# Halves of the probabilities in one matmul in all heads, and a new order of the stick-breaking work on VectorE

## What is computed

```
def stick_breaking_attention(q, k, v):
        z = jnp.einsum('bqhd,bshd->bhqs', qb, kf) * dh ** -0.5
        causal = (spos[None, :] < tpos[:, None])[None, None]
        log_beta = jax.nn.log_sigmoid(z)
        log_keep = jnp.where(causal, log_beta - z, 0.0)
        between = lax.cumsum(log_keep, axis=3, reverse=True) - log_keep
        a = jnp.where(causal, jnp.exp(log_beta + between), 0.0)
        return jnp.einsum('bhqs,bshd->bqhd', a, vf).astype(q.dtype)
```

## Time and profile before

| | |
|---|---|
| median of three runs | 738.01 us (737.94 to 738.75) |
| the profiled execution | 738.18 us, its span 736.4 us |
| TensorE clock granted, mean | 0.999 of full |
| TensorE matmul busy | 729.9 us, 99% of the span |
| VectorE busy | 595.8 us, 81% |
| ScalarE busy | 466.1 us, 63% |
| GpSimd busy | 257.9 us, 35% |

### The profile page before, as it was taken

How to read it: one execution, slowest core, us unless ns; L and a number is a source line. 1 busy time by engine, 2 the same in 40 slices (tenths; PEclk the granted TensorE clock), 3 DMA queues, 4 the chain that set the end, 5 groups by cost and what they waited for, 6 DMA issues and landing times.

```text
span 736.4 us, 11132 instructions
## 1 busy us (share of the span) xinstructions
PE 729.9 (99%) x3881; PEld 628.3 (85%) x3881; DVE 595.8 (81%) x838; ACT 466.1 (63%) x733; POOL 257.9 (35%) x204
## 2 busy tenths in 40 slices
PE   9999999999999999999999999999999999999997
PEld 7788888888888888888888999999999999888885
DVE  4979989978766777359998888888888888985787
ACT  5764177777858667654484756666666666764664
POOL 6837265976777878421003400000000000043201
PEclk9999999999999999999999999999999999999999
DMA  9662444222304223269971023333333354999914
GB/s 332 191 180 63 143 124 115 57 58 58 107 16 130 65 72 101 71 175 288 260 197 38 1 71 100 115 114 114 114 103 91 93 169 157 343 174 207 212 35 115
DMA packets 111520, 95.21 MB, mean 129 GB/s; under 512 B 3696, under 2 KB 91768, under 8 KB 111480
## 3 DMA queue, kind: packets, MB, share of 16 engines
q1 hardware_dynamic: 104920, 78.96, 34.5%
q0 software_dynamic: 6368, 15.73, 11.6%
q10 hardware_dynamic: 192, 0.01, 0.0%
HBM read 84.97 MB, written 4.73 MB: 122 GB/s over the span
## 4 chain that ended last, share of the span: by engine, by line
PE 97%; DVE 2%; issue 1%; ACT 0%; POOL 0%; POOLq 0%; DVEq 0%
PE ps L1060 13%; PE ps L1147 12%; PE ps L712 11%; PE ps L713 11%; PE ps L714 11%; PE ps L1066 6%; PE ps L734 6%; PE ps L983 4%; PE ps L775 3%; PE ps L1050 3%; PE ps L1048 3%; PE ps L1049 3%; PE ps L922 2%; PE ps L934 2%; PE ps L1003 1%; PE ps L907 1%
## 5 line engine op out<-in xcount | busy, mean ns | idle before, releaser
L712 PE MATMUL ps<-h_both,w_hi 128*128 128x512 f32 (+1 forms) x288 | 110.6, 384 | 0.0
L713 PE MATMUL ps<-h_both,w_hi 128*128 128x512 f32 (+1 forms) x288 | 109.1, 379 | 0.0
L714 PE MATMUL ps<-h_both,w_lo 128*128 128x512 f32 (+1 forms) x288 | 109.1, 379 | 0.0
L1950 POOL DMA_DIRECT2D w_a<-in_w_down x12 | 15.3, 1533 | 249.7 <-DMA w_a<-in_w_down 227.4
L1864 POOL TENSOR_TENSOR w_lo<-raw,w_hi 128x1024 fp32r<-128x1024 f32 x30 | 78.3, 2612 | 29.9 <-ACT w_hi L1343 29.5
L714 PEld LDWEIGHTS ps<-h_both,w_lo 128*128 128x128 f32 x288 | 54.2, 188 | 10.2
L713 PEld LDWEIGHTS ps<-h_both,w_hi 128*128 128x128 f32 x288 | 54.3, 189 | 8.9
L712 PEld LDWEIGHTS ps<-h_both,w_hi 128*128 128x128 f32 x288 | 54.3, 188 | 9.0
L1147 PE MATMUL ps<-wr_hi,xd_hi 128*128 128x512 f32 x154 | 60.0, 389 | 0.0
L1147 PE MATMUL ps<-wr_lo,xd_hi 128*128 128x512 f32 x154 | 59.9, 389 | 0.0
L1147 PE MATMUL ps<-wr_hi,xd_lo 128*128 128x512 f32 x154 | 59.9, 389 | 0.0
(11 more groups left out here) (337 smaller groups left out, 2074.6 us busy)
## 6 DMA issues: line engine op xcount, KB each, us to landing
raw<-in_w_in SPq DMA_DIRECT2D x40, 512.0 KB, 4.5
raw<-in_w_gate_up SPq DMA_DIRECT2D x24, 512.0 KB, 3.9
raw<-in_w_gate_up SPq DMA_DIRECT2D x40, 256.0 KB, 4.3
w_a<-in_w_down SPq DMA_DIRECT2D x9, 768.0 KB, 6.1
w_a<-in_w_down POOLq DMA_DIRECT2D x9, 768.0 KB, 10.7
s<-in_w_out SPq DMA_DIRECT2D x3, 768.0 KB, 8.2
w_a<-w_a POOLq DMA_DIRECT2D x3, 768.0 KB, 13.4
x_t<-in_first SPq DMA_DIRECT2D x8, 256.0 KB, 6.7
```

What stands on the lines that cost most here:

```text
L712: mm(acc, whi_c, a_hi_, start=first, stop=False, skip_group_check=further)
L713: mm(acc, whi_c, a_lo_, start=False, stop=False, skip_group_check=further)
L714: return mm(acc, wlo_c, a_hi_, start=False, stop=last, skip_group_check=further)
```

## The change

Three things. `MERGED` goes, and with it the form of `attend` and of `sum_out` that heads 0 to 3 had: all heads take six matmuls and two additions. On VectorE `kept_after(i + 1)` goes behind `turned_lo(i)`, for the stick-breaking heads. And the last two rounds of the top-k stand behind heads 1 and 3 instead of 0 and 1 (`LAST_ROUNDS`), the mask behind head 5 (`MASK_AFTER`) instead of head 2.

```diff
--- before.py
+++ after.py
@@ -88,10 +88,12 @@
 
 
 FIRST_FILL = 16
-MERGED = 4
 STEPS = (5, 8, 1)
 ROUNDS = TOPK // 8
 FIRST_ROUNDS = 13
+
+LAST_ROUNDS = (1, 3)
+MASK_AFTER = 5
 SHARE = 256
 
 
@@ -99,11 +101,6 @@
 
     first = FIRST_FILL + i * sum(STEPS) + sum(STEPS[:part])
     return first, first + STEPS[part]
-
-
-def outs_added(heads):
-
-    return heads + max(0, heads - MERGED)
 
 
 def tiles_ended(first, end):
@@ -912,7 +909,7 @@
 
             pe.wait_ge(probs_done, i + 1)
             if i:
-                pe.wait_ge(att_out_done, outs_added(i))
+                pe.wait_ge(att_out_done, 2 * i)
             else:
                 pe.wait_ge(va_kept, TB)
                 pe.wait_ge(vb_kept, TB)
@@ -927,18 +924,11 @@
             pe.wait_ge(v_hi_done, i // 2 + 1)
             pe.wait_ge(v_lo_done, i // 2 + 1)
             pe.wait_ge(a_lo_done, i + 1)
-            if i >= MERGED:
-
-                for k, half, first in ((0, 0, 0), (0, 1, HALF), (3, 1, 3 * P), (1, 0, P), (1, 1, HALF), (2, 1, HALF)):
-                    a, n = PACK[TB - k] + first - k * P, (half + 1) * HALF - first
-                    ins = mm(out_bank(half)[:, :, HALF - n:HALF], v_both[:, i % 2, k, :], a_both[:, :, a:a + n],
-                             start=k == 0, stop=k == half + 1, skip_group_check=True)
-            else:
-                for k in range(TB):
-                    n, a = (TB - k) * P, PACK[TB - k]
-                    for p, pr in enumerate((a_hi, a_lo)):
-                        ins = mm(z(1, k * P, S), v_both[:, i % 2, k, :], pr[:, a:a + n],
-                                 start=k == 0 and p == 0, stop=k == TB - 1 and p == 1, skip_group_check=True)
+
+            for k, half, first in ((0, 0, 0), (0, 1, HALF), (3, 1, 3 * P), (1, 0, P), (1, 1, HALF), (2, 1, HALF)):
+                a, n = PACK[TB - k] + first - k * P, (half + 1) * HALF - first
+                ins = mm(out_bank(half)[:, :, HALF - n:HALF], v_both[:, i % 2, k, :], a_both[:, :, a:a + n],
+                         start=k == 0, stop=k == half + 1, skip_group_check=True)
             ins.then_inc(out_done, 1)
 
         fill(0, 6)
@@ -1393,16 +1383,13 @@
 
             sc.wait_ge(out_done, i + 1)
             if i:
-                sc.wait_ge(att_out_done, outs_added(i))
-            if i >= MERGED:
-                run(att_rest.rearrange("p (x n) -> p x n", x=2), out_banks(slice(HD, P), 0), ACT.Copy).then_inc(att_rest_done, 1)
-            else:
-                run(att_rest[:, :], ps[HD:P, 5, :], ACT.Copy).then_inc(att_rest_done, 1)
+                sc.wait_ge(att_out_done, 2 * i)
+            run(att_rest.rearrange("p (x n) -> p x n", x=2), out_banks(slice(HD, P), 0), ACT.Copy).then_inc(att_rest_done, 1)
 
         def out_hi(i):
 
             r, chunk = slice(HD * (i % 2), HD * (i % 2) + HD), (i // 2 + PAIRS) % KC
-            sc.wait_ge(att_out_done, outs_added(i + 1))
+            sc.wait_ge(att_out_done, 2 * (i + 1))
             run(o_hi[r, chunk, :], att_out[r, :], ACT.Copy).then_inc(o_hi_done, 1)
 
         def gate(slot):
@@ -2179,14 +2166,11 @@
             ve.wait_ge(att_rest_done, i + 1)
             if 2 <= i:
                 ve.wait_ge(o_lo_done, i - 1)
-            if i >= MERGED:
-                rest = att_rest.rearrange("p (x n) -> p x n", x=2)
-                tt(rest, out_banks(slice(0, HD), HALF), rest, ALU.add).then_inc(att_out_done, 1)
-                ve.wait_ge(att_out_done, outs_added(i) + 1)
-                tt(att_out[r, :].rearrange("p (x n) -> p x n", x=2), out_banks(slice(0, HD), 0), rest,
-                   ALU.add).then_inc(att_out_done, 1)
-            else:
-                tt(att_out[r, :], ps[0:HD, 5, :], att_rest[:, :], ALU.add).then_inc(att_out_done, 1)
+            rest = att_rest.rearrange("p (x n) -> p x n", x=2)
+            tt(rest, out_banks(slice(0, HD), HALF), rest, ALU.add).then_inc(att_out_done, 1)
+            ve.wait_ge(att_out_done, 2 * i + 1)
+            tt(att_out[r, :].rearrange("p (x n) -> p x n", x=2), out_banks(slice(0, HD), 0), rest,
+               ALU.add).then_inc(att_out_done, 1)
 
         def rest_out(i):
 
@@ -2207,12 +2191,11 @@
         best_eight(FIRST_ROUNDS)
         k_rest(2)
         for i in range(ALL):
-            if i + 1 < HEADS:
-                kept_after(i + 1)
-            elif i + 1 < ALL:
+            if HEADS <= i + 1 < ALL:
                 logits_and_max(i + 1)
             turned_lo(i)
             if i + 1 < HEADS:
+                kept_after(i + 1)
                 break_probs(i + 1)
             elif i + 1 < ALL:
                 normalise(i + 1)
@@ -2220,10 +2203,9 @@
                 k_rest(i + 3)
             if i < ALL - 1:
                 sum_out(i)
-            r = FIRST_ROUNDS + 1 + i
-            if r < ROUNDS:
-                best_eight(r)
-            elif r == ROUNDS:
+            if i in LAST_ROUNDS:
+                best_eight(FIRST_ROUNDS + 1 + LAST_ROUNDS.index(i))
+            elif i == MASK_AFTER:
                 mask_the_rest()
         rest_out(ALL - 2)
         sum_out(ALL - 1)
```

## The result

The changed kernel takes 743.88 us, the median of six runs (742.48 to 747.24), beside 738.43 for the kernel before (six runs, 737.94 to 740.26). The ratio is 1.0075 [1.0063, 1.0087]: slower by 5.5 us, well outside the 0.2%. The forecast was 744.4, with a range of 741 to 748.

A forecast was written before the change was run, and what follows sets the result against it. TensorE was taken to bound the kernel, until VectorE's new loop with GpSimd outlasts a head. Waits of 2.0 + 5.0 less 0.56 for the merge gave +6.4 us on 738.01: 744.4, range 741 to 748.

The forecast's parts named there:

- The loop: Transposes, `a_hi`, `turned_lo`, scan, `break_probs`, `k_rest`, `sum_out`, next transposes: 10.37 us undisturbed, 14.34 with GpSimd, against TensorE's 13.10.
- three insertions: GpSimd's `q_lo`, `o_lo`, `w_lo` hold up scan, `break_probs`, `k_rest` by 0.91, 0.98, 2.08 us: together 3.97, with 2.73 spare.
- 1.24 each in loops 2 to 5: TensorE's wait at the transposes in each of these loops, 4.96 us together.
- 2.0 in loop 1: Transposes of head 2 come at 142.56 instead of 140.55 us: TensorE waits 2.0 us.
- the scan waits for `q_lo`: VectorE's scan behind `turned_lo` is held by GpSimd's `q_lo`, 2.39 - 1.48 = 0.91 us per loop.
- only some loops wait: Rival: two of five loops escape waiting, about 742 us; 8 in 100.
- third rival: More goes wrong: loop 6 waits 1.2 to 1.7 us, six TensorE restarts cost 0.2 each; 747.3 us, 12 in 100.
- VectorE pays for it: For the merged matmul in heads 0 to 3, `sum_out` becomes two instructions instead of one, 1.40 us in all.
- The rounds and the mask: Moved on VectorE, they cost nothing; if cover were gone, 0.7 us in two heads, and at most 1.2 for the mask.
- Loop 0: `k_rest` and `sum_out` end at 127.2, TensorE wants it at 127.45: no wait, by 0.2 us.
- Loop 6: Only one short piece of GpSimd's bias-and-mask sum comes between, costed at nothing; 1.2 us more if all held `k_rest`.
- The clock: Rival: clock falls during TensorE's pauses, one head at half clock adds 13 us, 757 us; 2 in 100.

The follow-up runs named there:

- the scan ahead: Changed kernel with `kept_after(i + 1)` ahead of `turned_lo(i)` again, six matmuls and late rounds kept: 738.78 us.
- `k_rest` last: Changed kernel with `sum_out(i)` ahead of `k_rest(i + 3)`, run twice: 738.25 and 738.66 us.
- `q_lo` late: Changed kernel where GpSimd's `q_lo` also waits for `a_lo_done` of head i, i from 1 to 6, so the scan comes first: 739.18 us.
- nudged kernel: Changed kernel with an 8x32 memset and a wait for it ahead of the scan in the loops of heads 1 and 2: 747.84 us.
- the order alone: Kernel before with only the scan moved behind `turned_lo`, eight matmuls and one addition in heads 0 to 3, rounds as before: 742.51 us.
- the changed kernel's second: The changed kernel run again, nothing altered, for another profile of its waits: 743.58 us.
- the merge alone: Kernel before with `MERGED = 0`, so six matmuls and two additions in all heads, order and rounds as before: 740.7 us.
- both: Changed kernel with the scan ahead of `turned_lo` again and `sum_out` ahead of `k_rest` as well: 738.22 us.

## Why the prediction was right, point by point

**The mechanism was right.** The loop, its three insertions, and the place of the wait came as worked out. In the loops of heads 3 to 5 the records are 3.50 to 3.73, 2.33 and 2.78 against 3.74, 2.46 and 2.77 in the sum, and the waits behind them 1.27, 1.43 and 1.26 against 1.24. It is shown from three sides: with the scan ahead or `k_rest` behind nothing waits, and with `q_lo` behind 0.2 us of 4.0 is left.

**Two terms of the sum were mis-sized.** The sum gave 6.4 us, all of it in the heads' stage, and that stage grew by 4.2. First, "1.24 each in loops 2 to 5" and "2.0 in loop 1": loops 1 and 2 did not wait, which takes 3.2 us off. The step that failed is "the scan waits for `q_lo`", taken from head 5 for all loops. The kernel before already showed the difference, on GpSimd in heads 1 and 5:

```profile
128.41 4.38 POOL L1864 TENSOR_TENSOR w_lo<-raw,w_hi 128x1024 fp32r<-128x1024 f32 x1 [4.92 <-ACT w_hi L1343]
132.92 2.37 POOL L1757 TENSOR_TENSOR q_lo<-proj,q_twice 64x512 fp32r<-64x512 f32 x1
...
181.23 2.40 POOL L1864 TENSOR_TENSOR w_lo<-raw,w_hi 128x1024 fp32r<-128x1024 f32 x1 [3.63 <-ACT w_hi L1343]
```

In head 5 that `w_lo` is over at 183.63, and GpSimd is idle for 0.32 us before `q_lo` (183.95 in the earlier trace rows); in head 1 `q_lo` follows a `w_lo` without a pause. In the changed kernel's heads 1 and 2 that `w_lo` ends just too late. Head 6 has such a pair too, and there `q_lo` is ahead of the scan by 0.08 us (202.37 and 202.45). The nudged kernel shows that in head 1's loop this was all: with `q_lo` first, it waited 2.07 us, as the 2.0 said. So the rival "only some loops wait" was right in that two of five escape; it kept the 2.0 of loop 1, which was one of the two, and its 742 was still 2 us low.

Second, the sum left out the restart of TensorE. Ten transposes that had to wait take 1.28 us in the chain instead of 1.09. (In the timeline the record is 1.25 us long without a wait, but 0.16 of it lies beside the matmul ahead.) Heads 1 and 4 to 6 show it, 4 x 0.19 = 0.8 us; the prediction had it only in its third rival. Together: 1.27 + 1.43 + 1.26 + 0.76 - 0.52 = 4.2 us, which is what heads 0 to 7 grew by. The same sum holds for the order alone: 2.7 + 0.3 + 3 x 0.19 = 3.6, and 95.82 - 92.25 = 3.57.

**The rest of the 5.5 us, and luck.** The medians differ by 5.5 us, the heads' stage by 4.2. The spans of the profiled executions, 741.8 (the changed kernel's second) and 736.4 (before), differ by 5.4, and the traces say where the other 1.2 lie. The first transposes come 0.5 us later (114.85 and 114.33), and TensorE is that late already at 54 us, where both kernels have the same code; they lay between 114.2 and 115.8 us in the kernels that lose nothing. And the stretch from the start of the last `attend` to the end is 0.7 us longer (420.4 and 419.75): there TensorE waits once for `xd_lo`, 0.4 us, with a DMA of weights in the chain. The kernels with the scan ahead, with `k_rest` last and with `q_lo` late have this wait too (0.3 to 0.5 us, stretches of 420.3 to 420.6), and the kernel before, the merge alone, "both" and even the nudged kernel don't (419.7 or 419.75). So neither piece comes with the loss; what makes the wait for `xd_lo` come or not is open. The forecast of 744.4 for 743.88 was therefore closer than its sum deserved: 6.4 us stood for 4.2 in the heads, and some 1.2 us that it had not counted filled part of the gap. That part is luck.

**The merge.** Forecast 0.56 us for four heads, seen 0.52 (91.73 against 92.25). The estimate of 0.41 from the Trainium skill's page ("TensorE: Matmul & The Clock Gate") is too low by 0.1; three kernels without the loss (scan ahead, `k_rest` last, both) gave 0.51 to 0.53. But "VectorE pays for it" was priced only inside the new loop; in the old order it costs two waits of 0.9 and 1.0 us, unless the rounds are moved.

**The rounds and the mask** cost nothing that the traces show, as said. What moving them buys shows beside the merge alone: without it `attend` waits in two heads, and heads 0 to 7 take 94.22 us instead of 91.73. **Loop 0** had no wait in the list, but its margin of 0.2 us was used up: head 1's transposes took 1.28. **Loop 6**: one short piece came between, `k_rest` was 1.11 and nothing waited. **The clock** stayed full in the heads of the changed kernel; it fell once there in the nudged one, with a loss of 1.65 us where that rival had 13.

**The rule of the skill.** The prediction set the trace's order of service against a page that does not say who goes first. Another one says more: the Trainium skill ("SBUF — State Buffer", SBUF: two separate sides) calls the port pair that the two engines share an exclusive lock, which a GpSimd instruction, or one of VectorE with two SBUF inputs, keeps for its whole length if it starts first, while the other is fully blocked. The runs agree: the scan is ahead by 0.06 us and takes 2.81, or behind by 0.10 and takes 3.86. That a waiting GpSimd instruction goes ahead of VectorE's next one, on which the second and the third insertion rest, is read from the traces alone (2.33 and 2.78 behind the scan's 3.73).

## What to carry to other kernels

Before moving an instruction of VectorE with two SBUF operands, lay its new place beside GpSimd's rows and count the GpSimd instructions that will be ready at each of its handovers. Each one can cost up to its whole length. An instruction that reads PSUM is not held up and lets one of them go by (`sum_out` here), so put such instructions of the critical path first, and the SBUF ones that nobody is waiting for last. Do the count for each turn of the loop, since a neighbour that one turn has and another hasn't can decide by less than 0.1 us.

## What the runs showed of the hardware

- A start 0.1 us later on VectorE changed the time of the whole by 4 us. In the profiled execution heads 0 to 7 took 101.34 us instead of 96.46, 1.65 of the 4.9 us by the clock and the rest by the order in which two engines came to SBUF. Without the nudge the order was the same in all three profiled executions.
- Scan, `break_probs` and `k_rest`, with two SBUF operands, take 2.81, 1.48 and 0.69 us alone and up to 4.89, 3.43 and 2.8 where a GpSimd instruction comes first. `turned_lo` and `sum_out`, which read PSUM, keep 1.49 and 0.68 in both cases.
- TensorE loses 0.19 us more than its wait at each restart on transposes (1.28 for 1.09). At `attend` it is some 0.3, an estimate: with the merge alone heads 0 to 7 grew by 1.97 us, where two waits less the merge give 1.91 - 0.52 = 1.39, and half of the rest is 0.3.
- One pause of 2.07 us was followed by 3.4 us at half the clock, while pauses of 1.26 to 1.43 us and one of 2.8 us were not. The cause is open.
